# First block's mixing stage reordered: recurrence among the attention projections, softmax units among the gates, the output gate as a flow of its own

## What is computed

```python
h = rms_norm(x, norm_mix[l])
proj = h @ w_in[l]
hq, hf, hi, hog, dq, dk, dv, gate_hg, gate_da = jnp.split(proj, splits, axis=-1)
f = lb + (1.0 - lb) * jax.nn.sigmoid(hf)
o_hg = hgrn2_chunked(heads_hg(hq), heads_hg(1.0 - f), heads_hg(hi), heads_hg(jnp.log(f)))
o_hg = rms_norm(o_hg, hg_out_norm[l]) * jax.nn.silu(heads_hg(hog))
y_hg = o_hg.reshape(B, S, HG_WIDTH) @ w_branch_hg[l]
qn = rope(rms_norm(dq.reshape(B, S, 2 * DA_HEADS, DA_HEAD), da_q_norm[l]), pos)
kn = rope(rms_norm(dk.reshape(B, S, 2 * DA_HEADS, DA_HEAD), da_k_norm[l]), pos)
...
o_da = diff_attention(qn[..., 0, :], qn[..., 1, :], kn[..., 0, :], kn[..., 1, :], v, lam)
o_da = rms_norm(o_da, da_out_norm[l]) * (1.0 - lam_init)
y_da = o_da.reshape(B, S, DA_WIDTH) @ w_branch_da[l]
mixed = jax.nn.sigmoid(gate_hg) * y_hg + jax.nn.sigmoid(gate_da) * y_da
x = x + (mixed @ w_out[l])
```

## Time and profile before

| | us |
|---|---|
| median of 3 runs | 2599.83 |
| lowest, highest | 2590.79, 2603.08 |
| profiled execution, its own time | 2602.66 |
| its span | 2600.5 |
| TensorE busy | 2217.0 (85%) |
| VectorE busy | 672.6 (26%) |
| ScalarE busy | 352.3 (14%) |
| mean granted clock of TensorE | 0.894 |

### The profile page before, as it was taken

The page is one execution under the profiler, slowest core; times in us unless marked ns, Lnnn a source line. Parts: engine busy times, 40 slices in busy tenths (PEclk is TensorE's granted clock), DMA queues, the critical chain, the costliest instruction groups (busy, mean ns, idle before and its releaser), DMA issues.

```text
span 2600.5 us, 26852 instructions
## 1 busy us (share of the span) xinstructions
PE 2217.0 (85%) x11637; PEld 1104.5 (42%) x11637; DVE 672.6 (26%) x1650; ACT 352.3 (14%) x675; POOL 122.5 (5%) x154
## 2 busy tenths in 40 slices
PE   7998789997788888679899887999999688888884
PEld 3445444453333333244566654444645433333331
DVE  2335820132010000031567545112113410000102
ACT  2201310010000000011222333100102100000001
POOL 4000000000000000000001000000000000000000
PEclk9998789997888888879899899999999788898887
DMA  5221011246999999650010100241423479999993
GB/s 173 75 87 65 1 60 69 84 199 271 427 427 427 426 426 424 252 176 24 3 27 2 67 2 1 81 162 65 162 78 124 159 333 427 428 426 425 425 425 151
DMA packets 92713, 524.28 MB, mean 202 GB/s; under 512 B 13013, under 2 KB 27530, under 8 KB 66986
## 3 DMA queue, kind: packets, MB, share of 16 engines
q1 hardware_dynamic: 77712, 483.43, 45.9%
q10 hardware_dynamic: 5130, 21.56, 2.2%
q0 software_dynamic: 9744, 17.47, 1.9%
HBM read 514.02 MB, written 25.17 MB: 207 GB/s over the span
## 4 chain that ended last, share of the span: by engine, by line
PE 67%; DMA 18%; DVE 8%; ACT 3%; issue 3%; POOL 1%; ACTq 0%; POOLq 0%; DVEq 0%
PE ps L198 61%; DMA SC<-xrows,ST 17%; PE ps L1310 2%; POOL ytab L1665 1%; PE ps L1332 1%; ACT SC L1401 1%; ACT SC L1405 1%; DMA SC<-ytab 1%; PE ps L363 1%; DVE X L1652 0%; PE ps L2599 0%; PE ps L2013 0%; DVE ST L1027 0%; DMA ytab<-SC,ST 0%; ACTq L398 0%
## 5 line engine op out<-in xcount | busy, mean ns | idle before, releaser
L198 PE MATMUL ps<-SC 64*64 64x64 f32 (+6 forms) x5744 | 745.2, 335 | 22.2 <-DVE SC L1620 13.0
L198 PE MATMUL ps<-RING,SC 128*64 128x512 f32 (+2 forms) x1904 | 690.4, 617 | 18.4 <-ACT SC L1401 12.5
L198 PE MATMUL ps<-XT,RING 128*128 128x512 f32 x1104 | 492.9, 600 | 4.8 <-DVE SC L1962 2.0
L198 PEld LDWEIGHTS ps<-SC 64*64 64x64 f32 (+3 forms) x5744 | 347.0, 149 | 264.2 <-issue 236.6
L198 PEld LDWEIGHTS ps<-RING,SC 128*64 128x64 f32 (+2 forms) x1904 | 242.9, 159 | 331.2 <-issue 331.1
L198 PEld LDWEIGHTS ps<-XT,RING 128*128 128x128 f32 x1104 | 208.1, 192 | 255.9 <-issue 252.3
L1310 PE MATMUL ps<-ident,SC 128*128 128x128 f32 x256 | 57.5, 397 | 131.9 <-DMA SC<-xrows,ST 131.9
L198 PE MATMUL ps<-XT,SC 128*64 128x512 f32 x320 | 162.8, 668 | 7.8 <-ACT SC L1401 7.8
L1445 DVE TENSOR_TENSOR SC<-SC,ps 128x512 f32<-128x512 f32 x32 | 22.0, 687 | 527.4 <-PE ps L198 527.4
L198 PE MATMUL ps<-RING,XT 128*128 128x512 f32 (+2 forms) x448 | 155.7, 502 | 0.0
L198 PE MATMUL ps<-SC,RING 128*128 128x512 f32 (+2 forms) x448 | 116.2, 433 | 0.0
(11 more groups left out here) (392 smaller groups left out, 1445.8 us busy)
## 6 DMA issues: line engine op xcount, KB each, us to landing
RING<-in_w SPq DMA_DIRECT2D x44, 2048.0 KB, 20.6
SC<-in_w SPq DMA_DIRECT2D x42, 2048.0 KB, 22.0
RING<-in_w_e_gate SPq DMA_DIRECT2D x17, 2048.0 KB, 24.1
SC<-in_w_e_up SPq DMA_DIRECT2D x17, 2048.0 KB, 19.5
RING<-in_w_in SPq DMA_DIRECT2D x16, 2048.0 KB, 8.0
SC<-in_w_e_down SPq DMA_DIRECT2D x16, 2048.0 KB, 21.7
RING<-in_w_e_up SPq DMA_DIRECT2D x15, 2048.0 KB, 18.3
RING<-in_w_e_down SPq DMA_DIRECT2D x11, 2048.0 KB, 22.4
```

Of the source, the lines that this page charges most:

```text
L198: return e.matmul(out, l, r, start=st, stop=sp, skip_group_check=True)
```

## The change

The recurrence's projections f, q and v now come first and alone. The four projections of the output gate leave HG and become a flow HO with one bank of its own (7). The recurrence's steps stand among DF's projections, the output-gate steps among DF's transpositions, and DH's units among the first branch's gate steps. The loads come in the new order. VectorE's product with the output gate waits for HO. The computation is the same.

```diff
@@ hg_p, hg_a, hg_v_
-        W.wait_ge(*slots.on("hog"))
-        for tt in range(NT):
-            b, free = c.take("g", tt)
...
+        e.memset(hg_S, 0.0).then_inc(*c.up("v", "zero"))
...
+        W.wait_ge(*HO.on("ev", "g", NT - 1))
         e.tensor_tensor(hg_o, hg_o, hg_og, A.mult).then_inc(*c.up("v", "o"))
...
+    HO = Flow(book, "ho", (7,))
+
+    def ho_p(e):
+        c = HO
+        W.wait_ge(*slots.on("hog"))
+        for tt in range(NT):
+            b, free = c.take("g", tt)
+            W.wait_ge(*free)
+            proj(e, b[:, :], lambda k: XT[:, k, tt * 128:(tt + 1) * 128], lambda k: w8("hog")[:, k, :], 8).then_inc(*c.up("p", "g", tt))
+            if tt == NT - 1:
+                c.also("p", "w", "hog")
+            yield
+        yield
+
+    def ho_a(e):
+        c = HO
+        for tt in range(NT):
+            W.wait_ge(*c.on("g", tt))
+            if tt >= 2:
+                W.wait_ge(*c.on("ev", "g", tt - 2))
+            e.activation(hg_E[:, tt % 2, :], c.at("g", tt)[:, :], AF.Tanh, scale=0.5).then_inc(*c.up("a", "eg", tt))
+            yield
+        yield
+
+    def ho_v(e):
+        c = HO
+        for tt in range(NT + 1):
+            if tt:
+                E = hg_E[:, (tt - 1) % 2, :]
+                W.wait_ge(*c.on("eg", tt - 1))
+                e.scalar_tensor_tensor(hg_og[:, tt - 1, :], E, 1.0, c.at("g", tt - 1)[:, :], A.add, A.mult).then_inc(*c.up("v", "ev", "g", tt - 1))
+            yield
...
         wload(e, "hf", w_in, 512, 512, (HG, ("w", "hf")))
+        wload(e, "hq", w_in, 0, 512, (HG, ("w", "hq")))
+        wload(e, "hi", w_in, 1024, 512, (HG, ("w", "hi")))
         wload(e, "dq", w_in, 2048, 512, (DF, ("w", "dq")))
-        wload(e, "hq", w_in, 0, 512, (HG, ("w", "hq")))
         wload(e, "dk", w_in, 2560, 512, (DF, ("w", "dk")))
-        wload(e, "hi", w_in, 1024, 512, (HG, ("w", "hi")))
         wload(e, "dv", w_in, 3072, 512, (DF, ("w", "dv")))
-        wload(e, "hog", w_in, 1536, 512, (HG, ("w", "hog")))
+        wload(e, "hog", w_in, 1536, 512, (HO, ("w", "hog")))
...
-        "mix1": [(HG, (0, 350), {"p": hg_p, "a": hg_a, "v": hg_v_}), (DF, (0, 230), {"p": df_p, "a": df_a, "v": df_v_}),
...
+        "mix1": [(HG, ((0, 0), (13 / 33, 82), (17 / 33, 100), (29 / 33, 188), (29 / 33 + 0.001, 208), (1, 224)), {"p": hg_p, "a": hg_a, "v": hg_v_}),
...
```

More of the change, by code:

```diff
@@ L633, in hg_a @@
             yield
[L634 to L640, removed]
         for tt in range(NT):
@@ L1690, in moe @@
         return c, {"s": s, "p": p, "a": a, "v": v, "g": g}, (RT, {"p": rt_p, "a": rt_a, "v": rt_v})
-    G1_FLOWS = [HG, DF, DH, DHO, G1]
+    G1_FLOWS = [HG, HO, DF, DH, DHO, G1]
     M0, moe0, (RT0, route0) = moe(0, G1_FLOWS, G1, [(G1, ("mix", 7))], ((3, 0, 4, 7, 1, 2, 5, 8, 6), {
@@ L2964, in build @@
     WEAVES = {
-        "mix1": [(HG, (0, 350), {"p": hg_p, "a": hg_a, "v": hg_v_}), (DF, (0, 230), {"p": df_p, "a": df_a, "v": df_v_}),
-                 (DH, (230, 360), {"p": dh_p, "a": dh_a, "v": dh_v}), (G1, (350, 600), {"p": lambda e: gate_p(e, gates1), "a": lambda e: gate_a(e, gates1), "v": lambda e: gate_v(e, gates1)}), (RT0, (543, 623), route0)],
+        "mix1": [(HG, ((0, 0), (13 / 33, 82), (17 / 33, 100), (29 / 33, 188), (29 / 33 + 0.001, 208), (1, 224)), {"p": hg_p, "a": hg_a, "v": hg_v_}),
+                 (DF, ((0, 82), (0.2, 112), (0.4, 144), (0.6, 176), (1, 210)), {"p": df_p, "a": df_a, "v": df_v_}),
+                 (HO, (176, 205), {"p": ho_p, "a": ho_a, "v": ho_v}), (DH, (212, 310), {"p": dh_p, "a": dh_a, "v": dh_v}),
+                 (G1, ((0, 226), (0.32, 325), (0.64, 407), (0.68, 407), (1, 462)), {"p": lambda e: gate_p(e, gates1), "a": lambda e: gate_a(e, gates1), "v": lambda e: gate_v(e, gates1)}),
+                 (RT0, (424, 479), route0)],
         "mix2": [(RE, (0, 77, 130, 183, 236), {"p": re_p, "a": re_a, "v": re_v, "g": re_g}),
```

## The result

The changed kernel took 2611.35 us (median of 6 runs, 2608.13 to 2613.5), the kernel before in the same session 2600.82 us (2590.79 to 2603.08). The ratio is 1.0046, 95% interval 1.0028 to 1.0064: some 10 us slower, of which 7 were forecast. It lies within 0.5%, and within the range.

A forecast was written before the change was run, and what follows sets the result against it. Between dense stretches of the first block's mixing stage, 66 us were waits and low clock. Walking the new order ended the stage at 569.1 us, plus 14 for clock 583, 7 later than before: 2607 us, range 2586 to 2626.

The forecast's parts named there:

- First twelve groups to 105.6: Start of first block's mixing stage: projections hf, hq, hi run from 23.2 to 105.6 us.
- Sixteen groups with the recurrence: Next part: groups 109.9 us, recurrence 23.4, turns 5.3, waits 9.4 for rotary steps and output gate; ends at 253.6 us.
- the low-clock case: Rival: interleaved stage mostly at 1.2 GHz, gate-group heads and output-gate groups too; 24 us later, 2624 us; chance 0.22.
- The recurrence's norm: Before hg_y's turns: TensorE still waits for the norm, 11.6 us against 11.45 before, reaching 265.2 us.
- Units: Softmax units in runs between gate groups: first five with turns 15.8 us, then 13.5, 6.6, 10.9, 11.9, 5.0; together 63.7.
- A gate group takes one wait away, not the run's: Among softmax units: a gate group covers one wait; units inside a run still wait, 4.8 us each at 512 keys.
- Attention norm: Behind gate group 5: product and norm chain make TensorE wait 8.0 us, 9.76 before; turns then take 1.7.
- Clock of the groups: Branch 0 gate groups after runs or norm: low clock costs 12.5 us, with half-speed small work 14 (0 to 27).
- The rest: Stage's end: eight branch 1 groups 82.4 us, wait 1.65, output projection and router 64; ends 569.1, or 583 with clock.
- Everything behind moves rigidly: Behind 576 us: all later work, expert stage first, shifts with the end of the mixing stage.
- the clock holds: Rival: dense groups between softmax units keep the clock at 1.00, stage ends at 569.1 us; 2593 us; chance 0.2.
- Waits are hidden: Rival: each run of units shrinks by a third (21 us), output gate waits for nothing (9); 2571 us; chance 0.08.

The follow-up runs named there:

- experiment 1: Changed kernel with the first branch's gate-and-branch groups moved back behind the softmax units, reordered projections kept; 2603.66 us, ratio 1.0023 to the kernel before.
- experiment 4: Changed kernel with eight whole gate groups, one behind every second softmax unit from the third on, instead of six; 2616.28 us, ratio 1.0058 to the kernel before.
- Experiment 2: Changed kernel with twelve unread 512-column matmuls on TensorE ahead of the wait for the recurrence's norm; 2610.19 us, ratio 1.0045 to the kernel before.
- experiment 6: Changed kernel with the recurrence's norm its own step, output-gate groups and q/k turns before hg_y's turns, two output-gate banks; 2590.11 us, ratio 0.9967 to kernel before.
- experiment 3: Changed kernel with each gate step cut into gate tile and branch tile, one half behind every unit from the third; 2584.58 us, ratio 0.9945 to kernel before.
- experiment 7: Changed kernel with half steps (from the second unit), recurrence's norm as own step, and attention norm treated likewise; 2552.2 us, ratio 0.9820 to kernel before.

## Why the forecast held, step by step

- **First twelve groups to 105.6:** 106.02, of which 0.35 is a later start.
- **Sixteen groups with the recurrence:** the four waits were 1.69, 3.22, 0.97 and 3.13, 9.0 together against 9.4, each at its place and on its releaser. The reason given for the third was wrong, though its length was right: VectorE had no rotary step ahead of that product but had been idle for 7.42 us, and what TensorE waited for was the tanh and the product themselves. What I left out is the clock: the low-clock case named the output gate's groups, the forecast itself did not. Two of them took 8.83 (3.4 us together), and the small work around the waits took 31.7 us for 28.7 (one recurrence step alone 4.84 instead of 3.26). With the later start that makes the 6.3 us by which hg_y's turns came late (271.56 against 265.2). It is the largest error of the sum, and 2.2 us of it are not in every run: in experiments 1 and 4 the same two groups took 7.13 and 8.0 us, and the stretch from 223.6 to 271.6 us was 45.8 us long instead of 48.0.
- **The recurrence's norm:** 11.53 for 11.6. Experiment 2 shows that it is not TensorE's, experiment 6 that most of it can be covered.
- **Units:** the first five with the turns 15.9 (taken 15.8); the runs 7.1, 11.5, 12.1, 13.5 and 6.2 for 6.6, 10.9, 11.9, 13.5 and 5.0. The sum is 66.4 for 63.7; 1.5 of this I had booked as half-speed small work. "A gate group takes one wait away, not the run's" was right, and experiments 3 and 4 are its proof from both sides.
- **Attention norm:** 7.96 for 8.0; turns 3.0 for 1.7.
- **Clock of the groups:** 8.4 us over groups 0 to 6 (1.8, 2.4, 2.2, 0, 0, 0.4, 1.6) for 12.5, or 14 with the small work. The price of one was near (2.0 for 2.5); four paid it in full, not five, and the two behind units of 384 and 512 keys paid nothing; ahead of the first of these the clock was at 1.00 (348 to 356 us).
- **The rest:** eight groups of 10.30, the wait of 1.65 and 64 us, as before. Stage end 588.5, forecast 583: the errors are 6.3 + 2.7 - 5.6 + 1.3, and 0.7 of small ones. So it is partly luck that the sum came within 5.4 us: the clock of the gate groups was booked too dear, and this pays for over half of what was left out before them.
- **Everything behind moves rigidly:** only roughly. The transpositions of the second block start 10.9 us later (1273.5 for 1262.6) and the span is 7.3 longer (2607.8 for 2600.5). But the stretch from there to the end, the same code in all kernels, takes 1331 to 1338 us in the nine profiles, so this is what single runs differ by. The medians' 10.5 us agree with the shift.

Of the rivals, *the clock holds* falls: its runs of units would have read 1.00. *Low clock throughout* had one of its two marks, the output gate's groups (in this profile), but three of the seven gate groups ran at full clock or nearly so, and 24 us are not there. *Waits are hidden* falls in this kernel, and experiment 7 shows what it was worth: the waits can be hidden, but by another cut of the steps, not by this order.

The Trainium skill's page "TensorE: Matmul & The Clock Gate", section "Loop structure matters more than you think", was quoted with the rule that matmuls whose evacuation runs beside them and that follow at once stay warm. Whole groups after two or three units mostly did not meet that: the head of the first was at 0.50 to 0.60 (284 to 292 us), though two of the seven ran at full clock. Half steps behind every unit came nearer to it, with waits of up to 1.5 us left, and the trace agrees with it: 1.00 from 260 to 400 us in experiment 7.

## What to carry to other kernels

A dense step hides one round trip of the chain it stands in, however long it is: cut the dense work so that a piece is about as long as the round trip (here 3.6 to 7 us for 3 to 5) and put one behind every link, rather than a block behind every second or third. Look then at what the dense piece itself asks of the other engines: its product stood ahead of the chain's next operation on VectorE, and that left 1.25 to 1.5 us open behind every branch tile. Before work is moved away to be hidden elsewhere, ask what it was hiding itself: here the recurrence had stood between the units, and with nothing in its place the reordering gained nothing (experiment 1). A norm that ends a flow should be a step of its own, with dense work already fed and waiting in spare banks behind it.

## What was not expected of the hardware

After a stretch at 1.00 in which TensorE was busy all but 1 us (experiment 2, 260 to 272 us), small work with waits of 0.4 to 1.4 us between kept it for less than 8 us: 1.00, 0.69 and 0.50 in the windows from 272, 276 and 280. Nor does an equal busy time mean an equal clock: in the window from 287 to 407 us TensorE was busy 105.1 us with eight uncut groups among the units and 105.4 with the half steps, at a mean clock of 0.90 and 0.98. (At the lower clock the same work is busy for longer, so the uncut kernel also did less in it.) What differed was how the work was spread.

And the clock behind a wait is not the same in every run. Behind the same 3.22 us of waiting the output gate's second group took 8.83 us in the profiles of the changed kernel and of experiments 2 and 3, and 7.13 in those of experiments 1 and 4, after the same instructions.
